# Turning raw x ahead of its norm, closing the last expert pair unsplit, and holding ring loads at the routing of a three-block kernel

## What is computed

```
for l in range(2):
    h = rms_norm(x, attn_norm[l])            # x * rsqrt(mean(x*x)) * gain
    proj = h @ w_in[l]                       # 1024 x 2472
    ...                                      # mLSTM, latent attention, spatial gating
    x = x + y @ w_out[l]
    x = x + hier_moe(rms_norm(x, ffn_norm[l]), ...)
# last block
h = rms_norm_2(x, norm_w)
proj = h @ w_in_2                            # 1024 x 6144
```

## Time and profile before

| | us |
|---|---|
| median of 3 runs | 1140.96 (1139.9 to 1141.71) |
| the profiled execution's own time | 1143.45 |
| its span, first to last instruction | 1141.6 |
| TensorE (PE) busy | 1065.0, 93% of the span |
| VectorE (DVE) busy | 405.1, 35% |
| ScalarE (ACT) busy | 274.1, 24% |
| GpSimd (POOL) busy | 103.4, 9% |
| moved by DMA | 282.33 MB, mean 247 GB/s |

### The profile page before, as it was taken

One profiled execution on the slowest core, in us unless ns is written; L12 is line 12 of the kernel. 1 busy time (PEld: TensorE's weight loads), 2 busy tenths in 40 slices (PEclk: granted clock), 3 DMA queues, 4 the chain that ended last, 5 costly groups with the idle time before them and its releaser, 6 DMA issues.

```text
span 1141.6 us, 12870 instructions
## 1 busy us (share of the span) xinstructions
PE 1065.0 (93%) x4545; PEld 540.8 (47%) x4545; DVE 405.1 (35%) x982; ACT 274.1 (24%) x511; POOL 103.4 (9%) x151
## 2 busy tenths in 40 slices
PE   5999978999999888999969999999979999999898
PEld 3576643333333324776543333333334845555443
DVE  2262345433343331352454344443430112333220
ACT  3435321111111113254211111111120015454300
POOL 1220121000000002210220000000000100000000
PEclk9999997999999988999979999999989999998899
DMA  8627245999999995045258999999978248430000
GB/s 285 209 74 295 74 173 200 392 412 412 413 412 411 412 372 172 1 159 211 74 188 293 408 411 412 411 412 413 394 261 332 74 48 301 185 130 18 0 1 37
DMA packets 95595, 282.33 MB, mean 247 GB/s; under 512 B 15880, under 2 KB 29494, under 8 KB 87232
## 3 DMA queue, kind: packets, MB, share of 16 engines
q1 hardware_dynamic: 89760, 273.19, 63.3%
q0 software_dynamic: 5792, 8.58, 2.1%
HBM read 289.59 MB, written 4.72 MB: 258 GB/s over the span
## 4 chain that ended last, share of the span: by engine, by line
PE 72%; SPq 15%; DMA 6%; ACT 2%; DVE 2%; issue 2%; POOL 0%; DVEq 0%; ACTq 0%; PEldq 0%; POOLq 0%
PE bank L1380 13%; SPq L546 11%; PE bank L879 11%; PE bank L972 7%; PE bank L911 6%; PE bank L1159 5%; PE bank L986 5%; PE bank L842 4%; SPq L552 3%; DMA ring<-in_w 3%; PE bank L1501 3%; PE bank L1517 2%; PE bank L1397 2%; PE bank L831 2%; DMA ring<-in_w_in 1%
## 5 line engine op out<-in xcount | busy, mean ns | idle before, releaser
L879 PE MATMUL bank<-ring,arena 128*64 128x512 f32 x1024 | 230.8, 600 | 7.9 <-DMA ring<-in_w 6.2
L1380 PE MATMUL bank<-ring,xfT 128*128 128x512 f32 x320 | 147.3, 618 | 0.7 <-ACT xfT L1554 0.7
L879 PEld LDWEIGHTS bank<-ring,arena 128*64 128x64 f32 x1024 | 71.4, 138 | 143.7 <-issue 133.5
L911 PE MATMUL bank<-ring,arena 128*64 128x512 f32 x512 | 116.9, 599 | 0.0
L1380 PEld LDWEIGHTS bank<-ring,xfT 128*128 128x128 f32 x320 | 62.1, 198 | 78.9 <-issue 77.8
L972 PE MATMUL bank<-ring,xfT 128*128 128x384 f32 (+2 forms) x256 | 96.3, 530 | 2.7 <-ACT xfT L1554 1.4
L842 PE MATMUL bank<-arena 128*128 128x512 bf16 x384 | 93.3, 379 | 0.0
L1862 DVE TENSOR_TENSOR arena<-bank,arena 128x512 f32<-128x512 f32 x64 | 44.3, 692 | 128.3 <-ACT arena L1536 128.3
L1536 ACT ACTIVATE arena<-bank 128x512 bf16<-128x512 f32 x64 | 38.2, 597 | 190.1 <-PE bank L911 190.1
L972 PEld LDWEIGHTS bank<-ring,xfT 128*128 128x128 f32 x256 | 48.4, 193 | 42.9 <-issue 25.3
L1532 ACT ACTIVATE arena<-bank,arena 128x256 f32<-128x256 f32 x32 | 15.2, 474 | 217.2 <-PE bank L879 217.2
(11 more groups left out here) (366 smaller groups left out, 1133.6 us busy)
## 6 DMA issues: line engine op xcount, KB each, us to landing
ring<-in_w SPq DMA_DIRECT2D x256, 512.0 KB, 13.3
ring<-in_w SPq DMA_DIRECT2D x64, 1024.0 KB, 13.4
ring<-in_w_in SPq DMA_DIRECT2D x14, 2048.0 KB, 14.9
ring<-in_w_in SPq DMA_DIRECT2D x8, 1536.0 KB, 16.1
ring<-in_w_out SPq DMA_DIRECT2D x6, 2048.0 KB, 7.7
ring<-in_w_in SPq DMA_DIRECT2D x2, 1696.0 KB, 13.7
x_store<-x POOLq DMA_DIRECT2D x4, 512.0 KB, 6.2
ring<-in_w_up_moba SPq DMA_DIRECT2D x1, 2048.0 KB, 18.8
```

Of the source, the lines that this page charges most:

```text
L879: ins = pe.matmul(bank[5][CELL * e:CELL * (e + 1), :], xg[:, par, 4 * h + k, at:at + CELL], view[:, e, :, k, :], start=(h == 0 and k == 0) ...
L911: ins = pe.matmul(bank[5 + n][CELL * e:CELL * (e + 1), :], turned[:, par, c, CELL * e:CELL * (e + 1)], down_view(s)[:, e, c, n * HALF:(n + ...
L1380: ins = pe.matmul(dst[:, :], xfT[:, k, t * P:(t + 1) * P], w[:, k, :], start=(k == 0), stop=(k == KD - 1))
```

## The change

1. **Raw x is turned.** At the start of both mixers and of the last block TensorE turns x itself, as soon as it is there, without `rstd` and gain. ScalarE (tile 0, 8 copies of 128x128) and VectorE (tile 1, `gain_turned`, 2 of 128x512) multiply the gain in by a per-partition column `gain_cols` while they copy out of PSUM. `rstd` is applied to the products when they leave PSUM: as a scale in ScalarE's copies, or, where tokens run along the row, through `rstd_row`, a 128x256 tile that two matmuls of TensorE spread (`spread_rstd`, bank use `rs`) and VectorE copies. The copies of q, k heads (4 a layer) and of qb, kb (4) go from ScalarE to VectorE. The squares come behind the turned copies.
2. **Start.** SP loads the identity first (129 columns), x and the gain columns; TensorE frees the ring slots at once; the rest of the constants (GpSimd) waits for x.
3. **Routing.** SP waits for the landing of the first gathered rows before it loads ring0 (and behind it ring1). TensorE multiplies 20 times by zeros after the slot table, turns the rows, and makes the gate tables behind that.
4. **Layer end.** The last pair is not split: ScalarE copies it as f32 to `y_rest`, and TensorE closes the four banks with one f32 product each (`close_banks`). VectorE's `overflow` moves from ahead of pair 0 to ahead of pair 14, and TensorE's read of its count to ahead of pair 15.

```
@@ sync
+            sp.dma_start(consts[:, 0:FIRST_CONSTS], io["consts"][:, 0:FIRST_CONSTS]).then_inc(loaded_first, 16)
+            sp.dma_start(x[:, 0, :], io["x"][0, 0:P, :]).then_inc(loaded_x[0], 16)
+            sp.dma_start(gain_cols[:, 0:DEPTH, :], io["attn_norm"]).then_inc(loaded_first, 16)
+            sp.dma_start(gain_cols[:, DEPTH, :], io["norm_w_2"]).then_inc(loaded_first, 16)
+            sp.dma_start(x[:, 1, :], io["x"][0, P:2 * P, :]).then_inc(loaded_x[1], 16)
...
+                    if h == 1 and par == 1 and first_rows is not None:
+                        sp.wait_ge(rows_landed[0], first_rows)
                     sp.wait_ge(frees[s], used(s))
@@ tensor
+            def close_banks(l):
+                q = (l + 1) * PAIRS - 1
+                for t in range(NT):
+                    for n in range(2):
+                        if t == 0:
+                            pe.wait_ge(main["high_ready"], 2 * q + n + 1)
+                        ins = pe.matmul(bank[2 * t + n][:, :], last_hot[:, t * P:(t + 1) * P], y_rest[:, n, :],
+                                        start=False, stop=True, skip_group_check=True)
...
             def turn(m):
                 for t in range(NT):
-                    pe.wait_ge(xf_ready, NT * m + t + 1)
+                    if m == 0:
+                        pe.wait_ge(loaded_x[t], 16)
+                    else:
+                        pe.wait_ge(x_tile_ready if t == 0 else x_ready, PER * m)
                     for half in range(2):
...
-                pe.wait_ge(gates_ready, l + 1)
-                by_slot(bank[7], lane_hot, ...
+                add_zeros(20)
                 q0 = l * PAIRS
+                pe.wait_ge(exp_wanted, l + 1)
                 pe.wait_ge(rows_landed[0], l * LAYER_ROWS + 16)
                 for half in range(2):
                     gather(half, 0, main, bank[4 + 2 * half])
+                pe.wait_ge(gates_ready, 2 * l + 1)
+                by_slot(bank[7], lane_hot, ...
...
-                pe.wait_ge(main["low_ready"], 2 * (l + 1) * PAIRS + 2)
-                last_combine(acc_done, True, freed[DOWN[1]])
+                close_banks(l)
@@ vector, last block
+                src = full(dve, plan, "rs")
+                step(dve.tensor_copy(rstd_row, src[:, 0:SEQ]))
...
+                for a, u in enumerate(("qb", "kb")):
+                    for half in range(2):
+                        name = u + "AB"[half]
+                        src = full(dve, plan, name)[:, :].rearrange("p (i s) -> p i s", i=2)
+                        dve.scalar_tensor_tensor(s_qkbT[:, a, 2 * half:2 * half + 2, :], src,
+                                                 1.0 if a else float(S_DIM) ** -0.5, row, ALU.mult, ALU.mult)\
+                           .then_inc(left(plan, name), 1)
                 dve.wait_ge(loaded_second, 4 * 16)
                 dve.memset(s_rel[0:S_HEADS, 32:33], NEG).then_inc(rel_ready, 1)
```

261 lines of the change are left out of this document (149 added, 112 removed).

## The result

The changed kernel takes 1126.34 us, the median of 4 runs (1124.19 to 1129.79). The kernel before, run beside it, takes 1140.43 (4 runs, 1136.27 to 1141.71). The ratio is 0.989, with a 95% interval of 0.9867 to 0.9914: faster by 9.8 to 15.2 us. The forecast was 1120.2 with a range of 1112 to 1128, so the time lies in the range, in its upper part, and the gain is 14.1 us between the medians where 20.8 were expected. The profiled execution of the changed kernel is its fastest, 1124.19 us, and that of before was slower than its median, 1143.45; between these two lie 19.3 us. Much of this study is about why the two differences are so far apart.

The account below looks back on a forecast made before the run. TensorE was taken as the bound, except that expert stages end with the stream of loads. Terms 5.0 + 3.2 + 0.5 + 2.1 + 8.5 + 2.5 - 1.0 = 20.8 us took the median 1140.96 to 1120.2, range 1112 to 1128.

Parts of the forecast that it names:

- What bounds the kernel: Whole kernel: expert stages end when the stream of loads ends; everywhere else TensorE is the bound, with four holes.
- Start: Kernel start: unit 2 lands between 10.5 and 12.1, unit 3 at 24.9 instead of 29.89; gain 5.0 us, ends 4 and 6.
- The second rival: Start: unit 2 shares its time with other loads, leaving 2.5 of 5.0 us; cold second seam takes 2.5: 1125; chance 0.16.
- Routing: Ahead of the experts: held ring loads let the gather go earlier, stream starts at 172.5; gain 3.2 us layer 0, 2.1 layer 1.
- the same 5.4 us: Layer 0 expert stream: first bytes and gaps beyond its bytes at 412 GB/s, assumed unchanged after the change.
- Seam between the layers: Layer 0 to 1: mixer starts 6.6 us behind the last product, not 15.5, then waits 7 us for mixer loads; gain 0.5.
- The first rival: Seam between the layers: mixer loads are no bound, so 8.4 to 10 us more are gained, 1111; chance 0.14.
- Seam to the last block: Layer 1 to last block: 15.1 us become 6.6, gaining 8.5, plus 2.5 from a clock that stays up; 11.0 us.
- Behind kb: Last block: `rel_ready` now comes behind VectorE's copy of kbB and the memset; 1.0 us lost, between 0.7 and 1.2.
- the ends of the terms: Whole sum: the terms' high and low ends, said to give 27 and 12 us of gain, 1114 and 1129.
- The third rival: Routing: the held loads, 4.19 MB, cost more than they give; both layers lose 24.4 us, total 1149.9; chance 0.04.
- the last one: Last seam: short holes let the clock fall all the same, 1122.7, inside the range; counted within the forecast's 0.66.

Follow-up runs that it names:

- e5_nohold: Changed kernel without SP's wait for the first gathered rows, so the held ring loads go out ahead of the routing again; 1125.64 us, ratio 0.9859.
- e8_consts: Changed kernel with GpSimd issuing the rest of the constants behind the landing of unit 2 instead of x; 1124.66 us, ratio 0.9861.
- e3_warm: Changed kernel plus 12 small products on TensorE between x's first transposes and unit 2's first product in layer 0; 1126.81 us, ratio 0.9891.
- e7_nobranch: Changed kernel without TensorE's program for overflowing cells and the branch around it; 1125.98 us, ratio 0.9878.
- e2_mixer_early: Changed kernel with layer 1's 16 mixer loads issued after three of the six units of w_in instead of all six; 1115.24 us, ratio 0.9788.
- e12_before: Kernel before the change, with layer 1's mixer loads issued behind three units of w_in; 1140.59 us against 1140.18, ratio 1.0001.
- e9_split: Changed kernel with each layer's last combine split again into bf16 words, remainders and 12 products; 1128.39 us, ratio 0.9898.

## Why the prediction was right, and where it was not

**What bounds the kernel** was right: TensorE outside the expert stages, the stream at their ends. e5_nohold, whose pair 0 starts up to 3 us later without effect, shows it directly.

**Start, 5.0 expected, 1.4 found (2.3 in the profile).** This step failed, by more than its low end of 4. Three things were in it. Unit 2 was to be begun by 12.1; it is begun between 11.8 and 14.2, and the constants, which I named for the upper end, show no part in it (e8_consts). The first products were taken at 11.62 us; behind a hole of 3.5 us they ran at half clock:

```profile
14.00:16.00 2.00, 2.00 (x4) 0.97 (x3) 0.56 (x3) 0.00 (x0) 0.00 (x0) 0.50 0.80 221
...
18.00:20.00 2.00, 2.00 (x7) 1.10 (x6) 1.69 (x10) 0.00 (x0) 0.00 (x0) 1.00 1.00 388
```

and took 13.32. And "unit 3 lands between 24 and 25.5" was unit 3 by its own bytes; e3_warm, where TensorE was there first, shows it landing at 28.1, and the 1.6 us of small products between the units were left out. The second rival, the start that gains little, came true in its first half, though not by the causes I gave: it left 2.5 us of the 5.0. Its second half, a cold last seam, did not come. Its 1125 is nearer to the measured 1126.3 than my 1120.2. The rule on turns between queues (Trainium skill, DMA: Bandwidth & Descriptors, Queues, rings and completion order) pointed to the constants. At the start no run shows its price, but e5_nohold agrees that queues share: the store of x, issued at 160.1, holds the gather until 170.4 when ring loads go beside it, and landed in 3.0 us without them.

**Routing, 3.2 and 2.1 expected, 2.0 and 3.0 found.** The sizes are right and the reason is not. The store takes 3 us with the hold, the gather goes 5.5 us behind the router's end where it was 8.7, pair 0 starts 3 us earlier: all as said. But the step from there to the gain failed: that the stream "starts at 172.5" and so ends earlier did not follow, since e5_nohold without the hold ends as early. The sum of the stream's bytes also left out 0.52 MB, GpSimd's load of the next gain, and carried its 1.3 us over in "the same 5.4 us" of first bytes and gaps; the change takes this load out of each stage, which by the rows at pair 14 is 1.3 of the 2.0 and of the 3.0. That the terms came out near was luck in this sense.

**Seam between the layers, 0.5 expected, 0.0 found.** Right but for the hole of 3 us behind the branch, which was in no term: the mixer started 9.1 us behind the last product instead of 6.6. The loads landed at 440.56, 36.3 us behind the last expert load (36 expected). The expected 7 us of wait were 4.3 here and 7.96 in e7_nobranch, because the hole behind the branch took the first 3; the clock's price, 2.1 expected, is the 1.3 to 1.9 us of a unit 3 in 15.2 to 15.8. The first rival (the loads are no bound) is refuted, and its price, 8.4 to 10 us, is what e2_mixer_early gained when its condition was made true.

**Seam to the last block, 11.0 expected.** From 853.58 to 837.60 and from 30.24 to 27.70: 15.98 and 2.54, less the 7.57 by which the stage ended earlier, are 10.95. In e12_before the same two were 14.7 instead of 15.1 and 29.27 instead of 30.24, so the profiled pair is a favourable one. The clock stayed up at this seam in every profile with the unsplit combine, where the longest hole was 1.2 us, and fell in e9_split behind a hole of 3.28. The advice to keep holes short (Trainium skill, TensorE: Matmul & The Clock Gate, Why this matters for your kernels) agrees with both.

**Behind kb, 1.0 expected,** 0.9 for the wait, and 0.45 for the two spreading products, which I had at nothing.

**Profile and median.** The last sentence of the sum took the median as 2.5 us under the profiled execution. Before, that was so; the changed kernel's profile happened to be 2.2 us under its median. Of the 6.1 us by which 1120.2 is too low, 3.6 come from the start, and some 2 from the last block, whose gain is 8.0 in the means (10.0 expected) and 12.0 in the profiled pair. For the profiled execution the forecast was 1122.7, 1.5 off, but only because the clock's chance there covered what the start had missed. Two slips of the working changed little: the ends of the terms add up to 13.1 us at the low side, not 12, and 94.1 MB at 412 GB/s are 228.4 us, not 228.6. So the forecast lay in its range by the width of the range and by errors that in part made up for each other; what held as a mechanism are the two seams and the wait behind kb.

The third rival (the held loads cost more than they give) and the last one stayed out: pair 0 is earlier, and the clock did not fall at the last seam.

## What to carry to other kernels

When a change lets an engine arrive earlier, look at once at what it needs next and at that load's place in its queue: here a reordering that was worth nothing before the change was worth 10 us behind it, where the change itself was worth 14. Where a stream of loads is the bound, add up the bytes of every queue: a gain load of 0.52 MB on another engine's queue stands with 1.3 us in each expert stage. A term for a stage that several waits bound in turn must be summed to its end (unit landing, clock, the small products between, the next landing), since curing the first only exposes the second. And where single executions differ by several us through the clock, read each stage from the profiles of all kernels that left it alone.

## What the runs showed of the hardware that I had not expected

- At a branch that skips a block of code TensorE stood 2.0 to 3.4 us at the seam between the layers beside ring loads, 1.1 there in e2_mixer_early at a DMA share of 0.32, 0.6 to 1.2 at the last seam at a full share, and not at all with the branch and its body removed (e7_nobranch). What makes it long or short was not found.
- The changed kernel had its half-clock stretches in the last block at other places in two executions (5.1 and 6.8 us of clock lost), and the kernels with the same last block lost from 3.4 to 10.2 us, with the block's time 289.0 to 294.5 us. What sets them off there was not found.
- In e7_nobranch unit 2's first products took 13.16 us, against 11.62 at full clock, although the granted clock reads 1.00 there. The trace's first record of the clock begins at 14.9 us in that execution, and time without a record is printed as 1.00; the products' steps go from 0.71 to 0.36 us at just that point. So at the start of a trace a 1.00 need not mean full clock; the products' own steps tell.
- When TensorE waits for the stream, a pair of experts takes 15.9 us, not the 15.3 that 6.29 MB at 412 GB/s make. Some 0.13 MB of gathered rows a pair are 0.3 of the 0.6 us, as an estimate; the rest has no row.
